# Latent attention and within-chunk products moved into one block, step copies moved to ScalarE, unused products at both borders

## The reference

```python
def step(state, inp):                       # rwkv7_scan, one position
    r_t, w_t, k_t, v_t, a_t, b_t = inp
    sa = jnp.einsum('bhvk,bhk->bhv', state, a_t)
    state = (state * w_t[:, :, None, :] + sa[..., None] * b_t[:, :, None, :]
             + v_t[..., None] * k_t[:, :, None, :])
    return state, jnp.einsum('bhvk,bhk->bhv', state, r_t)
...
    p = jax.nn.softmax(jnp.where(causal, sc, NEG_INF), axis=-1)     # mla_mixer
    outs.append(jnp.einsum('bhqk,bkhd->bqhd', p.astype(v.dtype), v[:, :q1]))
...
    y = jnp.concatenate([y_rwkv.astype(x.dtype), y_mla.astype(x.dtype)], axis=-1)
    x = x + y @ w_out[l]
```

## Time and profile before

| | us |
|---|---|
| median of 3 runs | 2288.95 |
| the three runs | 2288.28, 2288.95, 2304.92 |
| profiled execution | 2304.18 |
| its span, first to last instruction | 2302.4 |
| PE busy in the span | 2245.1 |
| DVE busy | 1698.5 |
| ACT busy | 1065.2 |
| POOL busy | 549.2 |

### The profile page before, as it was taken

The page is one execution under the profiler, slowest core; times in us unless marked ns, Lnnn a source line. Parts: engine busy times, 40 slices in busy tenths (PEclk is TensorE's granted clock), DMA queues, the critical chain, the costliest instruction groups (busy, mean ns, idle before and its releaser), DMA issues. The chain is left out here.

```text
span 2302.4 us, 39319 instructions
## 1 busy us (share of the span) xinstructions
PE 2245.1 (98%) x14848; PEld 1989.7 (86%) x14848; DVE 1698.5 (74%) x2879; ACT 1065.2 (46%) x1411; POOL 549.2 (24%) x226
## 2 busy tenths in 40 slices
PE   7999999999999999999999899999999999999997
PEld 6888998888888988899999787788888888888886
DVE  7688568885888488788878645778888885456886
ACT  5454464444444554556545412444444443333444
POOL 4776631027766620200003301110000000000001
PEclk9999999999999999999999878999999999999999
DMA  7455445555544355554454100355555555555554
GB/s 253 156 176 179 142 163 188 192 179 187 179 174 168 144 181 185 183 197 158 155 173 170 46 2 20 110 183 187 193 184 184 188 192 183 184 191 190 182 214 169
DMA packets 69034, 384.93 MB, mean 167 GB/s; under 512 B 15088, under 2 KB 22768, under 8 KB 23984
## 3 DMA queue, kind: packets, MB, share of 16 engines
q1 hardware_dynamic: 68912, 383.22, 47.0%
HBM read 380.02 MB, written 3.18 MB: 166 GB/s over the span
## 5 line engine op out<-in xcount | busy, mean ns | idle before, releaser
L259 PE MATMUL ps<-opA,whi 128*128 128x512 f32 x2340 | 828.4, 394 | 1.4 <-POOL low L241 1.4
L229 ACT ACTIVATE whi<-raw 128x2048 fp32r<-128x2048 f32 x346 | 660.2, 1909 | 91.3 <-DMA raw<-weights_dram 89.5
L260 PE MATMUL ps<-opA,low 128*128 128x256 f32 x2496 | 672.2, 279 | 0.2 <-DVE opA L987 0.2
L234 DVE TENSOR_TENSOR low<-raw,whi 128x2048 fp32r<-128x2048 f32 x252 | 577.3, 2291 | 66.1 <-ACT whi L229 50.4
L241 POOL TENSOR_TENSOR low<-raw,whi 128x2048 fp32r<-128x2048 f32 x95 | 436.4, 4606 | 448.5 <-ACT whi L229 422.1
L259 PEld LDWEIGHTS ps<-opA,whi 128*128 128x128 f32 x2340 | 438.5, 187 | 102.0 <-issue 2.5
L260 PEld LDWEIGHTS ps<-opA,low 128*128 128x128 f32 x2496 | 468.0, 187 | 13.7 <-DVE opA L987 0.5
L259 PE MATMUL ps<-opB,whi 128*128 128x512 f32 x1260 | 455.8, 401 | 17.2 <-DVE opB L408 12.0
L260 PE MATMUL ps<-opB,low 128*128 128x256 f32 x1344 | 365.2, 282 | 0.0
L259 PEld LDWEIGHTS ps<-opB,whi 128*128 128x128 f32 x1260 | 239.4, 190 | 76.5 <-DVE low L402 10.4
L268 ACT ACTIVATE crossed<-ps 128x256 f32<-128x256 f32 x168 | 64.7, 385 | 515.5 <-PE ps L262 515.3
(11 more groups left out here) (394 smaller groups left out, 3037.2 us busy)
## 6 DMA issues: line engine op xcount, KB each, us to landing
raw<-weights_dram SPq DMA_DIRECT2D x350, 1024.0 KB, 4.8
bias_t<-table_dram SPq DMA_DIRECT2D x16, 384.0 KB, 6.0
hT<-xT_dram SPq DMA_DIRECT2D x4, 512.0 KB, 8.9
out_dram<-hT SPq DMA_DIRECT2D x4, 512.0 KB, 2.9
lora_g<-lora_dram SPq DMA_DIRECT2D x1, 1024.0 KB, 5.1
p_in<-pT_dram SPq DMA_DIRECT2D x2, 256.0 KB, 2.8
lora_wa<-lora_dram SPq DMA_DIRECT2D x1, 512.0 KB, 5.8
chunk_mats_dram<-compact SPq DMA_DIRECT2D x4, 128.0 KB, 3.2
```

What stands on the lines that cost most here:

```text
L229: act.activation(whi[:, v % RING, :], raw[:, v % RING, :], ACT.Copy).then_inc(hi_done.sem, 1)
L234: v_.tensor_tensor(wlo(v % RING, 0, width), raw[:, v % RING, 0:width], whi[:, v % RING, 0:width].bitcast(F32), ALU.subtract).then_inc(lo_d ...
L259: pe.matmul(*cross, start=start, stop=False)
L260: mm = pe.matmul(ps[:, b, 0:T], wlo(s, w0, w0 + P), op[:, k, 0:T], start=False, stop=False)
```

## The change

All stages stand in one block: `phase_mla` and `phase_within` return stages that go into the same `together` as those before and after them. What the block borders had ordered is ordered by semaphores.

- TensorE begins the attention on `ev_done`; GpSimd clears `lower` when the projections' products are done; VectorE waits for the causal mask's DMA; TensorE, not SP, waits for the triangles' DMAs.
- TensorE makes the first item's transposes and scores ahead of the last head's product with the values, VectorE its mask ahead of the last two stores. For that GpSimd makes the closing factors of pair 0 after the fourth head's output and those of pair 1 after the eighth's; the other pairs follow. The first step products wait for the last store.
- ScalarE makes the copy from `held` to `step_n`, one item later, between line 1927's read and the reads of the next item's transposes; VectorE waits for it before it writes `held` again.
- `keep_running` issues products of a weight unit with itself, 128x128 by 128x512, into a free PSUM bank; nothing reads them. There are three after the first scores, two before the first item's first product, two and two in the last item, where there are no transposes and scores of a next one, and eight after the last step products.
- In the chain, SP issues the gate weights' DMA when the last scores are done, ScalarE begins when the last step products are done, VectorE when the last copy is done.

The diff without the lines that only moved by an indentation:

```diff
-                sp.wait_ge(*mx["causal_in"](32))
...
-        def phase_mla():
+        def phase_mla(u_next, following):
...
+                pool.wait_ge(mm_done.sem, u_next)
                 pool.memset(lower[:, 16:32, :], 0.0).then_inc(mx["cleared"].sem, 1)
...
-                    sp.wait_ge(*mx["sol_in"](64))
...
+                pe.wait_ge(ev_done.sem, u_next + 2)
                 scores(0)
...
+                    if n == MLA_H:
+                        following.first_products(pe)
                     if n >= 1:
...
+                v.wait_ge(*mx["causal_in"](32))
                 biased(0)
...
+                    if n == MLA_H:
+                        following.first_mask(v)
                     if n >= 2:
                         store(n - 2)
...
+            def keep_running(pe, n, bank):
+                s = u_next % RING
+                for _ in range(n):
+                    pe.matmul(ps[:, bank, :], whi[:, s, 0:P], whi[:, s, 0:512], start=True, stop=True)
...
+            def first_products(pe):
+                pe.wait_ge(*ml["biased"](MLA_H))
+                transposed(pe, 0)
+                scores(pe, 0)
+                pe.wait_ge(hi_done.sem, u_next + 1)
+                keep_running(pe, 3, 0)
...
                 for pair in range(RW_B):
+                    if pair < 2:
+                        pool.wait_ge(*ml["outT"]((MLA_H // 2, MLA_H)[pair]))
...
+                pe.wait_ge(*mx["sol_in"](64))
                 for n, (pair, sc) in enumerate(items):
+                    if n == 0:
+                        keep_running(pe, 2, 0)
                     pe.wait_ge(*wi["masked"](n + 1))
...
                     if more:
                         transposed(pe, n + 1)
+                    else:
+                        keep_running(pe, 2, 2)
...
                     if more:
                         scores(pe, n + 1)
+                    else:
+                        keep_running(pe, 2, 2)
...
+                        elif half == 0:
+                            pe.wait_ge(*ml["stored"](MLA_H))
...
+                keep_running(pe, 8, 2)
...
+                def step_out(n):
+                    pair, sc = items[n]
+                    act.wait_ge(*wi["mn_read"](2 * n + 2))
+                    act.activation(step_n[:, pair, sc, :, :], held[:, :, :], ACT.Copy).then_inc(wi["held"].sem, 1)
...
                     act.activation(tokA[:, y, :, DH:P], ...).then_inc(wi["G_read"].sem, 1)
+                    if n:
+                        step_out(n - 1)
                     if n + 1 < len(items):
                         tokens_read(n + 1)
...
+                step_out(len(items) - 1)
...
+                    if n:
+                        v.wait_ge(*wi["held"](n))
                     for half in range(2):
...
-                        v.wait_ge(*wi["mn_read"](2 * n + 2))
-                        v.tensor_copy(step_n[:, pair, sc, :, :], held[:, :, :]).then_inc(wi["held"].sem, 1)
-                        v.wait_ge(*wi["held"](n + 1))
...
+                sp.wait_ge(*wi["sc"](2 * RW_B))
                 sp.dma_start(lora_g[:, :, :], lora[:, 1:3, :]).then_inc(no["lora"].sem, 16)
...
+                act.wait_ge(*wi["mn"](4 * RW_B))
                 act.activation(op[:, 12:16, 0:T], y_mla[:, 4:8, :], ACT.Copy).then_inc(ch["mla_hi"].sem, 1)
...
+                v.wait_ge(*wi["held"](2 * RW_B))
                 v.tensor_copy(state[:, 1, :, :], step_n[:, :, 0, 0, :]).then_inc(ch["state"].sem, 1)
...
-        together(*stages, phase_mix(u, opnd[1], ready, summed))
+        stages += [phase_mix(u, opnd[1], ready, summed)]
...
-        phase_mla()
-        phase_within(u)
+        following = phase_within(u)
+        stages += [phase_mla(u, following), following]
...
-        together(chain, normed, mixed, up, down, up2, down2, phase_out(down2.summed))
+        together(*stages, chain, normed, mixed, up, down, up2, down2, phase_out(down2.summed))
```

More of the change, by code:

```diff
@@ new lines, in phase_mla, with _ @@
+            stage = Stage()
+            @stage.gpsimd
+            def _(pool):
+                pool.wait_ge(mm_done.sem, u_next)
+                pool.memset(lower[:, 16:32, :], 0.0).then_inc(mx["cleared"].sem, 1)
+            @stage.sync
+            def _(sp):
+                sp.wait_ge(*mx["cleared"](1))
+                for c in range(4):
+                    sp.dma_start(lower[32 * c:32 * c + 32, :, 32 * c:32 * c + 32],
+                                 chunk_mats[32 * c:32 * c + 32, :, :].rearrange("i s t -> s i t")).then_inc(mx["sol_in"].sem, 16)
@@ L1825, in program @@
+            return stage
         chunk_ends = place("chunk_ends", [P, RW_B, 2, 2, P], at=second + 8 * T)
@@ new lines, in scores @@
+            def scores(pe, n):
+                pair, sc = items[n]
+                t = slice(sc * P, sc * P + P)
+                if n:
+                    pe.wait_ge(*wi["masked"](n))
+                for h in range(2):
+                    r = slice(DH * h, DH * h + DH)
+                    pe.matmul(ps[:, 3 + h, 0:P], a_gate[r, pair, t], r_[r, pair, t], start=True, stop=True)
+                    pe.matmul(ps[:, 3 + h, P:2 * P], k_[r, pair, t], kk[r, pair, t], start=True, stop=True)
+                    mm = pe.matmul(ps[:, 3 + h, 2 * P:3 * P], k_[r, pair, t], r_[r, pair, t], start=True, stop=True)
+                mm.then_inc(wi["sc"].sem, 1)
@@ new lines, in _ @@
+            @stage.vector
+            def _(v):
+                for n, (pair, sc) in enumerate(items):
+                    t = slice(sc * P, sc * P + P)
+                    if n + 1 < len(items):
+                        masked(v, n + 1)
+                    v.wait_ge(*wi["ry"](n + 1))
+                    v.tensor_tensor(r_[:, pair, t], ps[:, 5, 0:P], r_[:, pair, t], ALU.add)
+                    v.tensor_copy(kk[:, pair, t], ps[:, 5, 3 * P:4 * P]).then_inc(wi["ry_read"].sem, 1)
+                    if n:
+                        v.wait_ge(*wi["held"](n))
+                    for half in range(2):
+                        v.wait_ge(*wi["mn"](2 * n + half + 1))
+                        for c in (2 * half, 2 * half + 1):
+                            v.scalar_tensor_tensor(step_m[:, pair, sc, c, :], eye2[:, :], pc[:, pair, 4 * sc + c:4 * sc + c + 1], ps[:, 6 * half + c % 2, 0:DH],
+                                                   ALU.mult, ALU.add)
+                            ins = v.tensor_copy(held[:, c, :], ps[:, 6 * half + c % 2, DH:P])
+                        ins.then_inc(wi["mn_read"].sem, 1)
```

368 lines of the change are left out of this document (162 added, 206 removed).

## The result

The changed kernel takes 2279.95 us (median of 11 runs, 2274.88 to 2283.84), the kernel before 2288.87 (11 runs beside it, 2285.16 to 2304.92). The ratio is 0.9943, 95% interval 0.9927 to 0.996: faster by 9 to 17 us, less than 1%. Its profiled execution took 2274.88 us, span 2273.1, mean granted clock 0.995; it is the fastest of the eleven, while the profiled execution of before (2304.18) is near the slowest of that kernel.

The account below looks back on a forecast made before the run. The prediction took TensorE as busy nearly everywhere, with a long half-clock stretch in the items. Its terms, 0.3 − 0.3 + 2.4 + 18.8 + 2.2 + 1.6 = 25.0, off 2304.18 gave 2279.2 us, range 2265 to 2291.

Parts of the forecast that it names:

- start: Start of the attention: a semaphore in place of the block border lets TensorE begin earlier, gain 0.3 us.
- Pair 0 on GpSimd: Closing factors made during the attention: two GpSimd operations can hold VectorE, 0.3 us lost, bounds 0 to 1.2.
- First item: Border from attention to items: first product at about 1299.5 instead of 1301.92, gain 2.4 us; unused products cost some 0.6.
- Items: Fifteen items at full clock: gain 18.8 us, from half clock and some 1.8 for line 1958's VectorE copy, held 4.91 us.
- Step copies: Sixteen copies moved to ScalarE within the items: 0.7 us of slack faces at most 0.42, cost nothing.
- Tail: Last item's first product to the chain's first: 6.8 us instead of 9.0, gain 2.2.
- Chain's first step: Start of the chain at full instead of half clock: 4.8 us instead of 6.4, gain 1.6, bounds 0 and 2.
- Against the median: Whole kernel: the median run already lacks most of the items' loss, so the gain on it is 9.8 us, 0.43%.
- Another cause of the spread: Rival, whole kernel: the median run pays the same half clock, so all 25.0 us come off, 2264 us; chance 0.14.
- A fall in the merged block: Rival, last heads or chain's first step: the clock falls again, costing 2.8 or 14.2 us, 2282 to 2293; chance 0.22.
- ScalarE as the bound: Rival, items: the copy and its wait use up 0.7 us of slack, costing 6.4 us, 2286; chance 0.06.
- Half clock for all items: Rival, items: clock falls before the first and stays at half, 4.0 us per item, 2343 for all sixteen; chance 0.05.

Follow-up runs that it names:

- kernel 1: The kernel before run again with no edit, to set time against mean granted clock for each run; median 2292.76 us (11 runs).
- kernel 2: The kernel before with only the sixteen step copies moved to ScalarE, borders kept, no unused products; ratio 1.0008 (0.9991 to 1.0026).
- kernel 5: The kernel before with only eleven unused products added at the border ahead of the items; ratio 1.0008 (0.9994 to 1.0023).
- kernel 9: The kernel before with step copies on ScalarE and eleven unused products at the border ahead of the items; ratio 0.9957, median 2284.14 us.
- kernel 3: The changed kernel with the step copies back on VectorE, one block and unused products kept; ratio 0.9948 (0.993 to 0.9966) to the kernel before.
- kernel 7: The changed kernel with step copies on VectorE and no unused products, so the one block alone; ratio 0.9963 (0.9951 to 0.9976) to the kernel before.
- kernel 10: The changed kernel with step copies on VectorE and GpSimd's weight splits delayed to hold a copy on purpose; ratio 0.9928 to the kernel before.
- kernel 8: The changed kernel with fourteen more unused products in TensorE's waits behind the chain and in the norm; ratio 0.9951, median 2279.63 us (6 runs).
- kernel 6: The changed kernel with the first item behind the last head again and the five unused products ahead of it out; ratio 0.9974, 2280.38 to 2296.53 us.
- kernel 4: The changed kernel without any of its seventeen unused products; ratio 0.9957 (0.9942 to 0.9973) to the kernel before.

## Why the prediction was right, and where it was not

**The bound** was read rightly: the items, with the half clock in them, are 18.9 of the 24.8 us that the profiled executions differ by from the attention on. **The sum:** 25.0 forecast from the profiled execution, 29.3 measured; 4.5 of these lie ahead of the attention, where executions differ anyway (1267.65 to 1274.82 in the table). From the attention on it is 24.8, against 24.7 forecast without the start. That these agree so well is partly luck: the chain gave 0.7 more than its term, first item, pair 0 and tail together some 0.5 less.

Term by term: *start* 0.3, measured 0.27 (idle 0.66 for 0.93). *Pair 0 on GpSimd* 0.3, measured 0.45. *First item* 2.4; the stretch from the attention's start gives 1.7, so with 0.45 added back 2.2. The unused products cost 0.77 there, not 0.6. *Items* 18.8, measured 18.9. *Step copies* 0, measured 0 (84.14 on either engine). *Tail* 2.2, measured 2.0, but made of something else: at full clock the old tail takes 7.18 (kernel 1), so 0.2 is the border's and 1.8 the clock's. *Chain's first step* 1.6, measured 6.41 − 4.41 = 2.0; to the norm 2.3.

**Against the median** the forecast was 9.8 us; medians give 8.9, the ratio 13 (9 to 17). The assumption behind it, that the spread is the length of the half clock, was shown by kernel 1. The size was low, then, and that 2279.2 lies within 1 us of the changed kernel's median (2279.95) is partly luck. An execution of before near its median (2290.35) has 91.12 us of items, 7.0 over the changed kernel, and 1.7 + 0.2 + 2.1 elsewhere, 11.0 in all; the forecast's 9.8 leave 18.8 − 15.2 = 3.6 for the items.

**The step that failed** is the one on what brings the long half clock. The prediction named the held copy as what stopped TensorE "before the second fall", and let the ScalarE copies remove it. Kernel 2 took the hold away and kept the fall; kernel 5 filled the border and kept a fall behind the hold; kernel 9 took both away and the time fell. There are two causes, each enough for a stretch at half clock in the items; kernel 9 shows it by its times, without a trace. Merging the blocks closes the border's wait, and in the three traces of the merged order with VectorE's copies (kernels 3, 7, 10) no hold is long enough to stop TensorE, so the ScalarE copies earn nothing there that these runs show. Nor do the splits run "at much the same time as before": the first begins 7.8 us behind the items' first product (1303.50 for 1295.69), before 5.0 (1306.95 for 1301.92), and so a copy meets its end. The Trainium skill, page "SBUF — State Buffer", section "SBUF: two separate sides", says that whichever engine starts first has the port pair for its whole instruction. The 3.26 us hold ends with one split, as it says; those of 4.91 and 7.68 us lasted through the next split too.

**The rivals.** Another cause of the spread: refuted by kernel 1. A fall in the merged block: not in the profiled execution, but kernel 8 had one of 3.4 us, 1.5 us lost, so it happens in some runs. ScalarE as the bound: items of 5.61 us, no. Half clock for all items: no. The changed runs spread over 9.0 us where before had 19.8.

**Open:** why a stretch at half lasts 6.8 and 34.1 us in one execution and 17 in another of the same kernel, why kernel 6 is as long as before in only half its runs, and why kernel 10 had no fall behind the chain where the changed kernel had two.

## What to carry over

When runs of one kernel differ by several us, set time against mean granted clock first: here that line explained the spread, and a profiled execution far from the median overstates a change. Undoing one part at a time can show no effect twice when two causes each suffice; take both away before calling either harmless. At the border here, reordering ready work into TensorE's waits did better than unused products in them: both kept the clock, but the attention's start to the first item took 27.26 us in kernel 4 and 29.74 in kernel 5. Unused products that outlast a wait cost time (0.77 us).

## What was not expected of the hardware

TensorE stayed at half clock for some 37 us while it read 36.95 of 38 us busy with small products (kernel 2). A VectorE copy that meets a GpSimd split took anything from 0.52 us, when it began 0.4 us ahead of the split's end, to 7.68 us through two splits; holds of up to 3.7 us cost the items at most 0.3 us. Kernel 10 waited behind the chain as the changed kernel did (both 0.96 us ahead of the norm's first sums) and had no fall there, where the changed kernel had two.
